# The second feed-forward product in seven products for eight, in blocks of 4, 4, 4, 4 and 6

## The reference

```
h2 = rms_norm(x, g_pre_ffn) * (1 + sc2) + sh2
gate, up = jnp.split(h2 @ w_ffn_in, 2, axis=-1)     # w_ffn_in 1024 x 5632
f = (jax.nn.silu(gate) * up) @ w_ffn_out            # w_ffn_out 2816 x 1024
x = x + g2 * rms_norm(f, g_post_ffn)
```

## Time and profile before

| | |
|---|---|
| median of 3 runs | 2071.51 us (2069.67 to 2072.68) |
| profiled execution, its own time | 2065.5 us |
| its span, first to last instruction | 2063.7 us |
| TensorE busy | 2030.6 us, 16241 matmuls |
| VectorE, ScalarE, GpSimd busy | 989.1, 624.9, 1066.5 us |
| matmuls of units (L1064) and of w_ffn_out (L1000) | 3024 and 2112 |
| mean granted clock of TensorE | 0.997 |

### The profile page before, as it was taken

The page is one execution under the profiler, slowest core; times in us unless marked ns, Lnnn a source line. Parts: engine busy times, 40 slices in busy tenths (PEclk is TensorE's granted clock), DMA queues, the critical chain, the costliest instruction groups (busy, mean ns, idle before and its releaser), DMA issues.

```text
span 2063.7 us, 38507 instructions
## 1 busy us (share of the span) xinstructions
PE 2030.6 (98%) x16241; PEld 1960.1 (95%) x16241; DVE 989.1 (48%) x1645; ACT 624.9 (30%) x1358; POOL 1066.5 (52%) x562
## 2 busy tenths in 40 slices
PE   8999999999999999999999999999999999999998
PEld 6999898999999999999989989889999999999997
DVE  5223466422257535647563235663223573647473
ACT  4111224110134333425532021340102343525253
POOL 0454454567763736353544534546687546354543
PEclk9999999999999999999999999999999999999999
DMA  9746222223351442323625352222232413223332
GB/s 360 259 136 62 62 76 59 67 80 93 87 178 42 128 128 83 94 81 103 220 60 178 61 64 73 62 62 75 82 97 85 157 42 93 82 83 91 94 93 77
DMA packets 299771, 211.93 MB, mean 103 GB/s; under 512 B 13728, under 2 KB 293840, under 8 KB 296400
## 3 DMA queue, kind: packets, MB, share of 16 engines
q1 hardware_dynamic: 292848, 205.94, 34.4%
q10 hardware_dynamic: 6752, 3.53, 0.9%
HBM read 204.65 MB, written 4.07 MB: 101 GB/s over the span
## 4 chain that ended last, share of the span: by engine, by line
PE 94%; DVE 2%; DMA 1%; ACT 1%; POOL 1%; issue 0%; SPq 0%; DVEq 0%; POOLq 0%
PE ps L972 43%; PE ps L1064 19%; PE ps L1000 13%; PE ps L1084 3%; PE ps L1090 2%; PE ps L1217 1%; DMA raw<-in_w_in 1%; PE ps L1132 1%; PE ps L1432 1%; PE ps L1596 1%; PE ps L1559 1%; PE ps L1447 1%; PE ps L1574 1%; PE ps L1260 1%; PE ps L1111 1%; PE ps L1626 1%
## 5 line engine op out<-in xcount | busy, mean ns | idle before, releaser
L972 PE MATMUL ps<-h_hi,hi_lo 128*128 128x288 f32 x3008 | 541.6, 298 | 0.3 <-POOL hi_lo L886 0.3
L883 POOL TENSOR_TENSOR hi_lo<-raw,consts 128x1024 fp32r<-128x1024 f32 (+1 forms) x124 | 237.2, 1913 | 466.9 <-PE ps L972 351.8
L972 PEld LDWEIGHTS ps<-h_hi,hi_lo 128*128 128x128 f32 x3008 | 446.5, 189 | 7.6 <-issue 5.3
L972 PE MATMUL ps<-h_lo,hi_lo 128*128 128x288 f32 x1504 | 322.3, 296 | 0.0
L886 POOL TENSOR_TENSOR hi_lo<-raw,hi_lo 128x1024 fp32r<-128x1024 f32 (+1 forms) x124 | 300.4, 2422 | 9.7
L899 POOL TENSOR_TENSOR a_lo<-raw,a_hi 128x512 fp32r<-128x512 f32 x108 | 160.0, 1482 | 269.3 <-ACT a_hi L2139 269.3
L972 PEld LDWEIGHTS ps<-h_lo,hi_lo 128*128 128x128 f32 x1504 | 242.8, 189 | 0.0
L1000 PE MATMUL ps<-yf_hi,fo_h 128*128 128x288 f32 x704 | 152.2, 298 | 3.0 <-DVE yf_lo L2314 3.0
L1900 ACT ACTIVATE tmp<-ps 128x576 f32<-128x576 f32 x60 | 39.1, 652 | 382.3 <-PE ps L972 382.3
L883 POOL TENSOR_TENSOR hx<-raw,consts 128x1024 fp32r<-128x1024 f32 x34 | 68.7, 2022 | 160.4 <-PE ps L1090 65.4
L1000 PE MATMUL ps<-yf_hi,fo_l 128*128 128x288 f32 x704 | 150.8, 296 | 0.0
(11 more groups left out here) (398 smaller groups left out, 4559.0 us busy)
## 6 DMA issues: line engine op xcount, KB each, us to landing
raw<-in_w_in SPq DMA_DIRECT2D x108, 512.0 KB, 3.8
ada<-in_w_ada SPq DMA_DIRECT2D x23, 2048.0 KB, 9.3
raw<-in_w_ffn_in SPq DMA_DIRECT2D x144, 256.0 KB, 3.1
raw<-in_w_ffn_out SPq DMA_DIRECT2D x32, 384.0 KB, 3.5
raw<-in_w_ffn_out SPq DMA_DIRECT2D x32, 320.0 KB, 3.2
raw<-in_w_out SPq DMA_DIRECT2D x16, 512.0 KB, 3.9
raw<-in_w_ffn_in SPq DMA_DIRECT2D x16, 512.0 KB, 3.9
raw<-in_w_br_mlstm SPq DMA_DIRECT2D x8, 512.0 KB, 3.4
```

The lines of the kernel that those rows point to most:

```text
L883: pool.tensor_tensor(hi, RAW[s][:, 0:size], ONES[:, 0:1].to_broadcast([128, size]), ALU.mult).then_inc(chunk_hi, 1)
L972: m = pe.matmul(o[:, h, :], a[:, k, c0:c0 + 128], mv(k, h), start=(k == 0 and begins), stop=(k == nk - 1 and a is wl))
```

## The change

The second product, too, is made in seven products for eight, for the first 16 y tiles; the last block of six stays as it is. A block of four y tiles is taken with pairs of output tiles: 2 x 2 tiles of y (halves of the tokens), 2 x 2 of weights. BLOCKS becomes (4, 4, 4, 4, 6), and the units run two y tiles ahead of the blocks (SPAIRS 2, 4, 4, 4, 4; 18 a layer as before). A pair has products in the order p1, p4, p6, p2, p5, p7, p3 of 6 matmuls each and takes two PSUM units, `ff{c}_{q}a` and `b`.

- For each block VectorE makes T sums of the y tiles (`out_t1`, `out_ts`; t3 in place of a half of y), ScalarE their high parts, GpSimd their low parts (`out_t_low` of 1728 elements, `out_t3_low` of 576). Low parts of whole y tiles stay on VectorE (`y_low`), at other places.
- For each pair SP loads the four tiles' blocks in three transfers in place of two; ScalarE and GpSimd make the parts of three blocks (`out_a_high`, `out_a_low`, 768 elements, for odd pairs as 512 and 256), VectorE four sums of 256 elements (`out_sums`), ScalarE and GpSimd their parts (`out_s_high`, `out_s_low`, 1024 elements).
- VectorE reads PSUM in six steps a pair (four of 288, two of 576 elements); p6 waits for the read of p1, p7 for that of p6, p3 for that of p5. For block 0 the four are copies.
- Modulation parts 2 and 3, `par+`, `wst+` and the token transposes move from the gaps of `fo` groups to those of `fi0_4` to `fi0_6`; in layer 0 the T sums of the first product (`t_add`) come after modulation part 3, whose buffer they share. The PSUM units of the feed-forward part are given out by a table.

```
-BLOCKS = (6, 5, 5, 6)
+BLOCKS = (4, 4, 4, 4, 6)
-SPAIRS = [b - PLAINP * (c == 0) for c, b in enumerate(BLOCKS)]
+SPAIRS = (2, 4, 4, 4, 4)
+OUT_PRODUCTS = ("p1", "p4", "p6", "p2", "p5", "p7", "p3")
...
 # TensorE
+                def out_begins(c, q, p):
+                    m, first = opair(l, c, q), f"ff{c}_{q}a"
+                    if p == "p1":
+                        pe.wait_ge(unit_of(l, first), empty(l, first))
+                        pe.wait_ge(f_alo, m + 1)
...
+                    elif p == "p4":
+                        if q == 0:
+                            pe.wait_ge(ft_lo, 2 * (LASTB * l + c) + 1)
+                    elif p == "p6":
+                        pe.wait_ge(f_slo, m + 1)
+                        pe.wait_ge(f_read, 4 * m + 1)
+                    elif p == "p2":
+                        pe.wait_ge(unit_of(l, f"ff{c}_{q}b"), empty(l, f"ff{c}_{q}b"))
...
+                    elif p == "p7":
+                        pe.wait_ge(f_read, 4 * m + 3)
...
+                    elif p == "p3":
+                        pe.wait_ge(f_read, 4 * m + 4)
...
+                    for k in range(2):
+                        for a, mv in ((wh, bh), (wh, bl), (wl, bh)):
+                            if k == 1 and a is wl:
+                                if i < 6:
+                                    out_begins(c, q, OUT_PRODUCTS[i + 1])
...
 # GpSimd, for each block
+                    for r in range(SPAIRS[c]):
+                        if 0 < c < LASTB and r + 1 == SPAIRS[c]:
+                            out_t_low(c)
+                        block_lo("a22", n0 + r)
...
+                    if c < LASTB:
+                        out_a_low(c, 0)
+                        if c == 0:
+                            out_t_low(c)
+                        out_s_low(c, 0)
+                        out_t3_low(c)
+                        for q in range(1, 4):
+                            out_a_low(c, q)
+                            out_s_low(c, q)
...
 # VectorE
+                def out_sums(c, q):
+                    m, s = opair(l, c, q), q % 2
+                    dve.wait_ge(f_raw[s], out_raws(l, c, q))
+                    if q < 2:
+                        dve.wait_ge(s_prod, nth_product(spairs(l, c + 1) - 1, "p3" if q else "p5"))
+                    else:
+                        dve.wait_ge(f_prod, nth_out(m - 2, "p3"))
+                    s1, s2, s3, s4 = (FSUM[s][:, i * 256:(i + 1) * 256] for i in range(4))
+                    a11, a12, a22, a21 = (RAW[s][:, i * 256:(i + 1) * 256] for i in range(4))
+                    tt(s1, a21, a22, ALU.add).then_inc(f_sum, 1)
+                    tt(s3, a11, a21, ALU.subtract).then_inc(f_sum, 1)
+                    dve.wait_ge(f_sum, 4 * m + 1)
+                    tt(s2, s1, a11, ALU.subtract).then_inc(f_sum, 1)
+                    dve.wait_ge(f_sum, 4 * m + 3)
+                    tt(s4, a12, s2, ALU.subtract).then_inc(f_sum, 1)
...
+                def follow(c, r):
+                    if c == LASTB:
+                        for j in {1: (16, 17), 2: (18, 19), 3: (20,)}.get(r, ()):
+                            y_low(j)
+                    elif c == 0:
+                        if r == 0:
+                            out_t1(c)
+                            out_ts(c, 0)
+                        else:
+                            out_ts(c, 1)
+                            y_low_first(c)
+                            y_low(2)
+                            y_low(3)
+                    elif r == 1:
+                        out_t1(c)
+                        out_ts(c, 0)
+                    elif r == 2:
+                        out_ts(c, 1)
+                        y_low_first(c)
+                    elif r == 3:
+                        y_low(4 * c + 2)
+                        y_low(4 * c + 3)
...
-                        if r:
-                            low_ys(c, r - 1, j0 + plain + r - 1, plain + r - 1)
...
                         if more:
                             weight_sum(1, c, r + 1)
                             weight_sum(2, c, r + 1)
+                        follow(c, r)
+                        if c < LASTB and not more:
+                            out_sums(c, 0)
                         gate_half(c, r)
                         if more:
                             weight_sum(3, c, r + 1)
                         up_tile(c, r)
                         if more:
                             sum_low(1, c, r + 1)
+                    if c < LASTB:
+                        out_sums(c, 1)
+                        read_p1(c, 0)
+                    gated_s(c, SPAIRS[c] - 1)
                     for u in (1, 2, 3):
                         free_unit(f"fs{c}_{u}")
...
+                    for q in range(4 if c < LASTB else 0):
+                        if q:
+                            read_p1(c, q)
+                        read_p4(c, q)
+                        if q == 3:
                             weight_sum(1, c + 1, 0)
+                        read_u(c, q)
+                        if q == 3:
                             weight_sum(2, c + 1, 0)
+                        read_p5(c, q)
+                        if q == 3:
                             sum_low(1, c + 1, 0)
+                        read_v(c, q)
+                        if q < 2:
+                            out_sums(c, q + 2)
+                        elif q == 3:
                             weight_sum(3, c + 1, 0)
+                        read_rest(c, q)
...
 # ScalarE, in a unit
+                        sums_in = c < LASTB and r == (1 if c == 0 else 2)
...
                         keep(1, c, r)
                         keep(2, c, r)
+                        if c < LASTB and not more:
+                            out_a_high(c, 0)
+                        if sums_in:
+                            out_t_high(c, 0)
                         if more:
                             block_high("a12", c, r + 1)
                             sum_high(1, c, r + 1)
                             sum_high(2, c, r + 1)
+                        if sums_in:
+                            out_t_high(c, 1)
                         silu(1, c, r)
+                        if sums_in:
+                            out_t_high(c, 2)
```

More of the change, by code:

```diff
@@ L231 @@
 P_FO = P_FFN + 2 * PLAINP
-NCH = P_FO + 8 * NB
+NCH = P_FO + 8
 assert NCH % 2 == 0
@@ L836, in _ @@
-                    for i in range(8):
-                        p = P_FO + 8 * c + i
-                        if i < 2:
-                            for b in ("a11", "a12") if i == 0 else ("a21", "a22"):
+                            if r:
+                                blocks_read(b, n0 + r - 1)
+                            elif c == 0:
+                                sp.wait_ge(chunk_split, split_count(l, P_FO - (2 if b[1] == "1" else 1)))
+                            else:
+                                out_blocks_read(c - 1, 2 if b[1] == "1" else 3)
@@ new lines, in input_tokens @@
+                def input_tokens(i):
+                    for x in XT_AFTER.get(i, ()):
+                        xt, c0 = f"xt{x}", slice(x * 128, (x + 1) * 128)
+                        act.wait_ge(done_by(xt), done(l, xt))
+                        act.activation(XTOK[:, :, c0], unit(l, xt)[:, 0:512].rearrange("p (t c) -> p t c", t=4), ACT.Copy)
+                        act.activation(XSTOK[64:128, c0], unit(l, xt)[64:128, 512:640], ACT.Copy) \
+                           .then_inc(unit_of(l, xt), 1)
@@ L2210, in _ @@
                             t_high(3, T3H, T3SUM)
+                        if 0 < c < LASTB and not more:
+                            out_t_high(c, 3)
                         sum_high(4, c, r)
@@ new lines, in taken, with read_p1 @@
+                def taken(c, dst, o):
+                    return tt(dst, o, dst, ALU.add) if c else dve.tensor_copy(dst, o)
+                def read_p1(c, q):
+                    m = opair(l, c, q)
+                    if c:
+                        for u in "ab":
+                            older = f"ff{c - 1}_{q}{u}"
+                            dve.wait_ge(unit_of(l, older), read(l, older))
+                    else:
+                        dve.wait_ge(t_sum, nth(t_sum, l, 3))
+                    dve.wait_ge(f_prod, nth_out(m, "p1"))
+                    taken(c, OMID[:, 2 * q, 0:HALF], unit(l, f"ff{c}_{q}a")[:, 0:HALF]).then_inc(f_read, 1)
```

613 lines of the change are left out of this document (407 added, 206 removed), and 4 rows, old and new, of the table AFTER.

## The result

The changed kernel takes 2215.37 us in the median (2213.74 to 2220.24), the one before 2070.59 (2068.64 to 2072.68) on the same chip: 1.0707 times as long, 95% interval 1.0688 to 1.0725. That is 145 us slower where +115 was predicted; 2215.4 lies in the range of 2095 to 2225 and 0.4 beyond the upper end of the likeliest case's own, 2215. It is nearer to the rival in which TensorE's clock falls (2207) than to the forecast (2186).

What follows compares the result with a forecast made beforehand. TensorE, busy 2030.6 of 2063.7 us, was taken as the bound. Stalls of 151.4 us less 25.5 saved gave +126, or +109 if VectorE keeps the port; +115 was taken: 2186 us, own range 2160 to 2215, overall 2095 to 2225.

Steps and rivals of the forecast that it cites:

- the rival in which TensorE's clock falls: 25 matmuls after the first pair's stall run at 1.2 GHz, 0.24 us each, costing 21 us: 2207; chance 0.14.
- moved work: Modulation parts, tokens, transposes: same matmuls between groups, 0.5 us a layer, bounds 0 and 3, for PSUM units ScalarE empties.
- A: Middle block, unit r=1: out_t1 and out_ts run first, gate_half is late; 1.8 us with restart, 0.7 without exclusion.
- B: Middle block, unit r=2: GpSimd idle, out_ts and y_low_first end at +9.4; 0.6 us, the same without exclusion.
- C: Middle block, unit r=3: out_t_low ahead of the a22 low part, sum_low(3) late for p7; 1.5 us, 0 without exclusion.
- D: Middle block, unit r=3: a_low(0), two y_low and out_sums(0) precede gate_half, p4 waits; 2.4 us with restart, 0 without exclusion.
- E: First pair: out_sums(1) alternates with GpSimd's low parts, p6 awaits read_p1; 3.8 us, 2.0 if VectorE keeps the port.
- F: After the first pair's stall: gated_s waits for a_low(1), p2's PSUM unit is freed late; 1.1 us, 0.1 without exclusion.
- G: Second pair: out_sums(2) precedes read_p1, p6 waits; 1.6 us without exclusion, 3.6 with a_low(2) in between.
- H: Third pair: out_sums(3) precedes the reads, with only the 0.7 us half of a_low(3); 2.2 us, 1.6 without exclusion.
- I: Every pair: read_p1 and read_p5 take 0.76 us where one product covers 0.66; 0.1 each, 0.8 us a block.
- block 0: E / T low parts: First block's first pair: low parts alternate with sums, 6.4 us (3.1 if VectorE keeps the port); p4 awaits out_t_low, 2.3.

Runs made afterwards that it cites:

- The memsets: Changed kernel with GpSimd's subtractions for the low parts of the T sums, t3 and pair sums replaced by memsets to zero; 2147.69 us.
- The kernel with memsets and both repairs: The memsets, plus ScalarE's a11 high part after the gate tiles and the third and fourth pairs' sums after the read of p4; 2110.61 us.
- kernel with memsets and another order: The kernel with memsets and both repairs, with products p1, p4, p5, p6, p2, p3, p7 in the second to fourth pair; 2101.07 us.

## Why the prediction was right, and where its sizes were off

That it is slower, by stalls behind VectorE that GpSimd lengthens, holds; so does the size of the idle time. Against 0.1328 us a matmul the stages of the two first blocks lose 37 us, of the six middle ones 112, of the two last 8; with 15 for the moved work and without 26 for the clock that is 146, against my 134 to 151. The profiled execution, for which I had 2180, took 2215.15, 35 more. Two terms that I had priced too low or put into a rival give 40 of that: the clock, 26, and the moved work, 14. The other stalls come to 131 where my +115 held 139 (between my two ends, 133 and 150), which takes 8 back; 3 stay open. In the medians the miss is 29 us, as the profiled execution before was 5 or 6 us faster than the median and the one after was not; I had carried those 6 us along. So the number lies as near as it does partly by luck: the stalls came out at the low end, and the rival's clock on top of them. By the prediction's own steps, block 1 of layer 0, idle and restart together (in brackets: E if VectorE keeps the port, G without exclusion):

```
step                        predicted    measured
unit r=0                    0            1.1
A  (r=1)                    1.8          1.7
B  (r=2)                    0.6          0.4
C  (r=3, before p7)         1.5          0.9
D  (r=3, before p4)         2.4          2.4
E  (first pair)             3.8 (2.0)    3.1
F  (p2's unit)              1.1          0 (0.5 where E is gone)
G  (second pair)            3.6 (1.6)    1.6
H  (third pair)             2.2          2.0
I  (reads, a block)         0.8          1.9 where nothing else waits
block 0: E / T low parts    6.4 / 2.3    5.4 / 2.5
moved work, both layers     1            15
clock                       0 (rival 21) 26
```

- **The saving** is as reckoned: 192 matmuls fewer.
- **A to D**: right in place and within 0.6 us in size. A stall at r=0 was missed: weight_sum(1) of the next unit is itself shut out by GpSimd, which I had not followed beyond gate_half.
- **E and the exclusion**: right, with E between its two ends. My sum put all exclusion, GpSimd's subtractions of the weight blocks included, at 115 - 27 = 88 us. The memsets take away three kinds of operation in it, with them part of the clock's loss, and some of GpSimd's length: 68, or 54 where they are cut into pieces. The share of the exclusion alone in that is not measured.
- **F and G**: too high. G gave a_low(2) the port between the sums; in the trace the sums ran back to back, and the stall is the bracketed 1.6. It is 3.0 and restart in the run with p4 repeated, where a_low(2) does meet the sums: a race, and not a step that can't happen. In the sum, H lacks the restart that G has. F lay hidden behind E, and is 0.5 where E is gone.
- **I**: it took the read of a bank to be covered but for 0.1 us and left out the restart, another 0.1 each time. Where nothing else waits it is 1.9 us a block in place of 0.8, and with p7 and p2 the short stops are 3.1, some 24 us in eight blocks: nearly the whole saving of 25.5. The kernel with memsets and both repairs loses another 44 us in its units, the waits for gate_half above all (27.4 us in the view of waits), and that is why it is still 40 us slower than before.
- **Moved work**: the step that failed was "the same matmuls between groups" with bounds of 0 to 3 a layer. I looked at what TensorE and VectorE do there and not at what stands ahead of gate_tile(2) in ScalarE's queue.
- **The clock** was a rival with a chance of 0.14; its condition came true, and the forecast's silent one, that the clock stays, did not. It should have been a term of the sum, which had stalls of 3.8 and 6.4 us in it. The rival's 25 matmuls of 0.24 us stood there without a row; behind E the runs show just these, and stalls elsewhere add to them. The Trainium skill ("TensorE: Matmul & The Clock Gate", "Why this matters for your kernels") warned of such gaps, and the rows at 0.50 agree with it.

Left open: the 6.6 us of waits for `h_lo` in the mixing part, which vary from run to run (3.5 in the kernel before, 3.8 to 7.2 in the others), and the 3 us above; one profile can't tell them from chance. Open too is how the 68 us of the memsets divide, and whether zeros as operands change anything for TensorE itself. That weight_sum(1) and not the load delays r=0 was read from the trace and not tried.

## What to carry to other kernels

Before a product is split into shorter ones, compare the length of one with the round trip of its reader: TensorE's end, VectorE's read, restart. Here 0.8 us of cover for a read that takes 0.76 lost 0.5 us a pair or more, and such short stops alone ate what the split saved; most cures moved a wait to another engine's deadline. Put stalls and what they do to the clock into one sum, and follow every queue that a moved step passes, ScalarE's too.

## What the runs showed of the hardware

- A stop of TensorE costs more than its idle row: about 0.24 us more for one of 1.00 us at a clock of 1.00. A start that came 0.05 us late (799.51, kernel with memsets and another order) was followed by one 0.11 late, 0.16 in all, and had no idle row.
- Behind the stall of 2.7 us (818.35) and that of 5.1 us (733.06) TensorE ran at 1.2 GHz (granted clock 0.50) for 25 matmuls each, some 6 us, and then at 2.4 again. In the kernel with memsets and both repairs, which has no listed stop over 0.3 us in its pairs, 12 us of busy time at the low level were left of 61.
- GpSimd's memset took 955 ns for 1024 elements and let VectorE's two-input operations run beside it; its subtraction of as many took 2.42 us and held them up until its end. Memsets of 151 ns each, one behind the other, overlap: 16 took 1.45 us.
